# Thirteen output-gate column tiles move from the input projection into the delta-rule stage

## The reference, cut to what matters

```python
proj = h @ w_in
aq, ak, av, dqkv, dz, dbeta, da, gates = jnp.split(proj, SPLIT_IDX, axis=-1)
...
o = o_fwd + o_bwd          # gated delta rule, once in each direction
...
g_a, g_b = jnp.split(gates, 2, axis=-1)
merged = jax.nn.sigmoid(g_a) * (attn_out @ w_attn_branch) + jax.nn.sigmoid(g_b) * (dn_out @ w_dn_branch)
```

## Time and profile before

| | |
|---|---|
| median of the runs | 2925.03 us |
| the profiled execution | 2921.28 us |
| its span, first to last instruction | 2919.2 us |
| mean granted TensorE clock | 0.941 |
| TensorE busy | 2599.4 us (89%) |
| VectorE, ScalarE, GpSimd busy | 1047.7, 808.6, 583.3 us |
| projection | 0 to 740 us |
| attention | 740 to 1016 us |
| delta rule | 1016 to 1434 us |
| merge, mix_out | 1434 to 1826 us |
| ff_in, ff_out | 1826 to 2919 us |

### The profile page before, as it was taken

The page is one execution under the profiler, slowest core; times in us unless marked ns, Lnnn a source line. Parts: engine busy times, 40 slices in busy tenths (PEclk is TensorE's granted clock), DMA queues, the critical chain, the costliest instruction groups (busy, mean ns, idle before and its releaser), DMA issues. The chain is left out here.

```text
span 2919.2 us, 33331 instructions
## 1 busy us (share of the span) xinstructions
PE 2599.4 (89%) x12792; PEld 2174.6 (74%) x12792; DVE 1047.7 (36%) x1372; ACT 808.6 (28%) x1223; POOL 583.3 (20%) x498
## 2 busy tenths in 40 slices
PE   6999999999799862878669796999999979998998
PEld 5888887888577652878658585888888858887887
DVE  4675035000588755664454332100000032224333
ACT  4343223010577630111120132311111142223221
POOL 3352155221000050212142132212222100000000
PEclk9999999999899985888769898999999989999999
DMA  4223213421232293446465544332323164336442
GB/s 142 73 83 94 72 62 121 132 74 69 111 129 97 81 289 116 159 162 202 136 191 169 180 170 173 130 90 72 90 72 90 57 209 133 101 129 213 169 152 104
DMA packets 313805, 372.00 MB, mean 127 GB/s; under 512 B 51560, under 2 KB 248808, under 8 KB 309096
## 3 DMA queue, kind: packets, MB, share of 16 engines
q1 hardware_dynamic: 189368, 274.57, 28.7%
q10 hardware_dynamic: 124336, 96.05, 10.1%
HBM read 250.93 MB, written 119.64 MB: 127 GB/s over the span
## 5 line engine op out<-in xcount | busy, mean ns | idle before, releaser
L2165 DVE TENSOR_TENSOR hid_lo<-ff_raw,hid_hi 128x1024 fp32r<-128x1024 f32 x96 | 113.9, 1222 | 836.1 <-ACT hid_hi L2129 836.0
L2075 PE MATMUL y_ps<-w_hi,hid_hi 128*128 128x512 f32 x768 | 301.5, 393 | 30.7 <-DVE w_lo L2159 19.8
L2075 PE MATMUL y_ps<-w_lo,hid_hi 128*128 128x512 f32 x768 | 300.2, 391 | 0.0
L2075 PE MATMUL y_ps<-w_hi,hid_lo 128*128 128x512 f32 x768 | 300.1, 391 | 0.0
L115 PE MATMUL proj_ps<-ht_hi,win_hi 128*128 128x512 f32 x888 | 260.6, 402 | 0.0
L115 PE MATMUL proj_ps<-ht_lo,win_hi 128*128 128x512 f32 x888 | 251.3, 391 | 0.0
L115 PE MATMUL proj_ps<-ht_hi,win_lo 128*128 128x512 f32 x888 | 250.4, 390 | 0.0
L115 PE MATMUL ff_ps<-ffx_hi,w_hi 128*128 128x512 f32 x768 | 217.1, 391 | 16.9 <-DVE ffx_lo L1944 16.9
L115 PE MATMUL ff_ps<-ffx_lo,w_hi 128*128 128x512 f32 x768 | 216.6, 391 | 0.0
L115 PE MATMUL ff_ps<-ffx_hi,w_lo 128*128 128x512 f32 x768 | 216.3, 390 | 0.0
L2129 ACT ACTIVATE hid_hi<-ff_raw 128x1024 fp32r<-128x1024 f32 x96 | 97.4, 1053 | 355.2 <-PE y_ps L2075 329.5
(11 more groups left out here) (225 smaller groups left out, 4196.6 us busy)
## 6 DMA issues: line engine op xcount, KB each, us to landing
ff_raw<-s_hid_s SPq DMA_DIRECT2D x96, 512.0 KB, 4.4
pack_in<-s_dn_s SPq DMA_DIRECT2D x24, 1024.0 KB, 6.6
s_hid_s<-ff_stage ACTq DMA_DIRECT2D x32, 768.0 KB, 4.3
win_raw<-in_w_in SPq DMA_DIRECT2D x39, 512.0 KB, 3.7
w_raw<-in_w_ff_in SPq DMA_DIRECT2D x32, 512.0 KB, 5.3
ff_raw<-in_w_ff_out SPq DMA_DIRECT2D x32, 512.0 KB, 5.4
s_gate_s<-proj_stage ACTq DMA_DIRECT2D x16, 768.0 KB, 3.2
k_head<-s_k_s SPq DMA_DIRECT2D x8, 1536.0 KB, 8.0
```

What stands on the lines that cost most here:

```text
L2075: mm = pe.matmul(acc[:, bank(u, t)], x[:, (t if opens(t) else kh), k], y[:, w], start=w == 0 and first == 0, stop=w == KF - 1 and first == 2)
L2165: dve.tensor_tensor(hlo[:, b, ks].rearrange("p k j -> p (k j)"), raw[:, r], f32(hhi[:, b, ks]).rearrange("p k j -> p (k j)"), ALU.subtract ...
```

## The change

`project` keeps the first 3 gate tiles (`EARLY_GATES`), 26 tiles in all; `GATING` becomes 14. The activations `ht_hi`, `ht_lo` stay in SBUF through `deltanet`, which now follows at once; `attend` comes after it. `deltanet` computes the other 13 gate tiles: 13 x 3 groups ("units") of 24 matmuls, into two banks of PSUM in turn. The stage is a list of segments (`ORDER`): 11 makes, 4 waiting segments, make 11, 4 waiting segments, 25 steps. Each gets a number of fill matmuls (`FILL`), which `fill` issues at fixed places in the segment: before and after a make, and at five places between the links of a step. ScalarE loads the weights (one raw buffer), evacuates units by sigmoid and stores them; GpSimd splits the weights at the beginning of segments. A step now belongs to one direction: step v is direction v % 2, chunk step v // 2, and its links are woven with the preparation of step v+1, of the other direction. Packs, triangles, inverses and outputs have one buffer per direction instead of two; the two banks of the inverse's growth are shared by the directions, the gates' two banks in `make` are no longer doubled. The inverse of batch 1 begins with 12 rounds ahead of the steps and goes on with two rounds at each of two places of steps 0 to 4, batch 2 at steps 6 to 13. The identity that an inversion starts from is loaded by SP instead of copied by GpSimd. In SP's order the triangle and the inverse of step v+2 are loaded apart from its pack, and the first triangles and packs come after the last store of `make`.

```diff
-             [("gate", i, GATE_COL + i * P) for i in range(2 * KD)])
+             [("gate", i, GATE_COL + i * P) for i in range(EARLY_GATES)])
...
-    GATING = N - 8
+    GATING = 14
...
+    GATES = range(EARLY_GATES, 2 * KD)
+    UNIT = 3 * KD
+    ORDER = ([("make", t) for t in range(11)] + [("wait", n) for n in range(4)] + [("make", 11)] + [("wait", 4 + n) for n in range(4)] +
+             [("step", v) for v in range(-1, STEPS)])
+    FILL = {"make": 10, "wait": 24, "step": 25}
...
+        def at(v):
+
+            return v % 2, v // 2
...
+        PRE = 12
+        WOVEN = {}
+        for v in range(5):
+            j = PRE + 4 * v
+            WOVEN[v] = [(1, j, min(j + 2, BLK - 1)), (1, min(j + 2, BLK - 1), min(j + 4, BLK - 1))]
+        for v in range(6, 14):
+            j = 4 * (v - 6)
+            WOVEN[v] = [(2, j, min(j + 2, BLK - 1)), (2, min(j + 2, BLK - 1), min(j + 4, BLK - 1))]
...
+                for v in range(2):
+                    load_low(v)
+                for v in range(2):
+                    load_pack(v)
+                for v in range(STEPS):
+                    if v == 5:
                         store_inverse(1)
                         load_blocks(2)
+                        sp.wait_ge(s["inv_stored"], 128)
+                        load_identity()
+                    if v == 14:
                         store_inverse(2)
+                    if v + 2 < STEPS:
+                        load_low(v + 2)
+                        load_inverse(v + 2)
+                        load_pack(v + 2)
+                    store_out(v)
...
+                def fill(seg, share):
+
+
+                    end = filled[seg] + int(round((filled[seg + 1] - filled[seg]) * share))
+                    while place[0] < end:
+                        x, n = divmod(place[0], UNIT)
+                        i, g = divmod(x, NG)
+                        k, first = divmod(n, 3)
+                        if n == 0:
+                            pe.wait_ge(s["w_ready"], i + 1)
+                            if x >= 2:
+                                pe.wait_ge(s["f_used"], x - 1)
+                        w, h = ((whi, ht_hi), (whi, ht_lo), (wlo, ht_hi))[first]
+                        mm = pe.matmul(ps[:, 6 + x % 2], w[:, i % 2, k], h[:, k, g * 512:(g + 1) * 512], start=n == 0, stop=n == UNIT - 1)
+                        if n == UNIT - 1:
+                            mm.then_inc(s["f_done"], 1)
+                        place[0] += 1
...
+                    if kind == "make":
+                        fill(seg, 0.5)
+                        if n == 0:
+                            sums()
+                        make(n)
+                    if kind == "step":
+                        now, after = n >= 0, n + 1 < STEPS
...
                         if now:
+                            state_products(n)
                         if after:
+                            grow_x32(n + 1)
+                        fill(seg, 0.24)
                         if now:
+                            solve(n)
+                        fill(seg, 0.4)
                         if after:
+                            grow_t32(n + 1)
                         if now:
+                            new_products(n)
                         if after:
+                            turn(n + 1)
+                        fill(seg, 0.64)
                         if after:
+                            grow_x64(n + 1)
+                        fill(seg, 0.84)
                         if after:
+                            grow_r64(n + 1)
+                    fill(seg, 1)
...
+                        act.activation(sig[:, u], ps[:, 6 + u], ACT.Sigmoid).then_inc(s["f_used"], 1)
+                        act.wait_ge(s["f_used"], x + 1)
+                        act.dma_start(io["gate_s"][GATES[i] * P:(GATES[i] + 1) * P, g * 512:(g + 1) * 512], sig[:, u]).then_inc(gate_stored[u], 16)
...
+                    pool.tensor_copy(whi[:, i % 2], raw[:]).then_inc(s["w_hi"], 1)
+                    pool.wait_ge(s["w_hi"], i + 1)
+                    pool.tensor_tensor(wlo[:, i % 2], raw[:], f32(whi[:, i % 2]), ALU.subtract).then_inc(s["w_ready"], 1)
...
-PHASES = [project, attend, deltanet, merge, mix_out, ff_in, ff_out]
+PHASES = [attend, merge, mix_out, ff_in, ff_out]
...
+        project(nc, io, ht_hi, ht_lo)
+        deltanet(nc, io, ht_hi, ht_lo)
```

More of the change, by code:

```diff
@@ L953, in deltanet, with view @@
[L953 to L959, removed]
-        ps = c.ps("dn_ps", [P, 8, 512])
+        def view(first, shape, of=arena):
+            n = int(np.prod(shape))
+            names = "abcd"[:len(shape)]
+            return of[:, first:first + n].rearrange(f"p ({' '.join(names)}) -> p {' '.join(names)}", **dict(zip(names, shape)))
@@ new lines, in deltanet @@
+        feat = view(0, (3, 2, DNW))
+        decay = view(3072, (2, 2, NH, P))
+        made = arena[:, 5120:10240].rearrange("p (v a h t) -> p v a h t", v=2, a=5, h=NH)
+        other_masks = view(5120, (2, 2, P))
+        made_in = view(0, (2, 2, NH, P))
+        r, x_last, v_new, state = (view(1024 * n, (2, NH, P), late) for n in range(4))
+        q_state = view(3072, (2, NH, P))
+        out = view(4096, (2, DNW))
+        pack = view(5120, (2, 4, DNW))
+        x_m = view(9216, (NH, HALF))
@@ L970, in deltanet @@
[L970 to L978, removed]
+        pack_in, qk_back, low_back, inv_back, out_stored, state_ready, gate_stored = (c.sems2(n) for n in (
+            "pack_in", "qk_back", "low_back", "inv_back", "out_stored", "state_ready", "gate_stored"))
@@ L980, in side, with scaled @@
+        def at(v):
+            return v % 2, v // 2
+        def scaled(v):
+            return len([w for w in range(v) if not last(w // 2)])
         def side(a, which, b):
@@ L1044, in load_inverse @@
-                def load_inverse(u):
+                def load_inverse(v):
+                    d, u = at(v)
                     sp.wait_ge(s["inv_stored"], 64 * (u // 4 + 1))
                     if u == 0:
[L1047 to L1055, removed]
@@ L1189, in _, with low @@
[L1189 to L1196 removed]
+                    heads(ps[:, 2 + b], lambda h: feat[:, t % 3, 0, h * P:(h + 1) * P], lambda h: feat[:, t % 3, 1, h * P:(h + 1) * P]).then_inc(s["qk_mm"], 1)
+                def low(d):
+                    return lambda h: made_in[:, d, LOW, h]
@@ new lines, in turn, with grow_x64 @@
+                def turn(v):
+                    d, u = at(v)
+                    pe.wait_ge(s["t_upd"], v + 1)
+                    for h in range(NH):
+                        tr = pe.transpose(ps[:, BA, h * P:(h + 1) * P], inv_in[:, d, 0, h], ident[:])
+                    tr.then_inc(s["turned"], 1)
+                def grow_x64(v):
+                    d, u = at(v)
+                    heads(ps[:, BD], low(d), lambda h: side(inv_in[:, d, 0], d, HALF)[:, h], HALF).then_inc(s["x64_mm"], 1)
@@ L1272, in _ @@
+                for u in range(2):
+                    act.wait_ge(gate_stored[u], sent[u])
             @block.vector
@@ L1453, in _ @@
[L1453 to L1473 removed]
+                        pool.wait_ge(pack_in[d], 16 * (u + 1))
```

632 lines of the change are left out of this document (335 added, 297 removed).

## The result

The changed kernel takes 2813.02 us (median of four runs, 2810.65 to 2814.03), against 2926.56 us for the kernel before beside it: a ratio of 0.9608, with a 95% interval of 0.9586 to 0.963. The profiled execution took 2812.34 us, its span is 2810.6 us, and the mean granted clock of TensorE rose from 0.941 to 0.956.

A forecast was written before the change was run, and what follows sets the result against it. The prediction took TensorE as the bound, idle or at a lower clock in the delta-rule stage: 2921.3 - 212.2 + 102.1 + 1 gave 2812, plus 2 for the median, 2814 us; range 2776 to 2868.

The forecast's parts named there:

- Removed: Projection: the 13 moved gate tiles' whole 212.2 us goes; the moved gating block costs 1 us.
- Steps: Delta-rule steps: TensorE is the bound, fill covering each link's read-back; 14.45 us per step, 346.5 us in all.
- Inverse waits: Steps: TensorE waits 9.4 and 9 us for inverses of batches 1 and 2, slow matmuls 2.5 each; together 23 us.
- GpSimd beside VectorE: Steps: weight splits hold VectorE through the shared SBUF port, mostly covered by slack; 3 us.
- The stage's beginning: Delta-rule stage before the steps: split, load and later triangle loads move the first step matmul from 1150.55 to near 1156.5.
- The end: End of the delta-rule stage: 4.3 us to the next stage's first issue, as before.
- A: Delta-rule stage: the two inverse waits vanish and the start does not grow; 2782 us, chance 0.18.
- B: Shared SBUF port: all 13 splits in series with VectorE, and VectorE with TensorE; 2856 us, chance 0.11.
- C: Steps: TensorE's clock stays at the earlier mean of 0.85, adding 61 us; 2875 us, chance 0.10.
- D: Steps: fill covers no wait, one direction at a time exposes each link; period 19.0 us, 2965 us, chance 0.07.
- E: Delta-rule stage: fill merely lengthens it by its own 212 us; 2925 us, chance 0.04.

The follow-up runs named there:

- e3: Changed kernel with SP's wait for batch 1's inverse to land, and the identity load, moved behind the loads of step 7: 2810.22 us.
- e7: e3 with the loads of step 7's triangle and inverse also put ahead of batch 1's stores: 2803.05 us.
- e9: Changed kernel with GpSimd's subtraction of each weight split cut into four pieces: 2808.57 us.
- e5: Changed kernel with GpSimd's subtraction of each weight split performed twice: 2838.36 us.
- e1: Changed kernel with all 16 gate tiles back in the projection and no fill in the delta-rule stage: 2918.79 us, 0.997 of the kernel before.
- e10: Changed kernel with step 7's loads first, batch 2 earlier, more fill in waiting segments, subtraction in pieces, first split behind the first gate products: 2789.59 us.

## Why the prediction was right, point by point

**Forecast 2814, measured 2813.02.** The sum held because its large terms are of one kind: matmuls counted and priced by spacing. That it came within 1 us is luck: the start is 3.7 us and the end 2.8 us longer than in the sum, and the way from the first step's matmul to the last output is 6.4 us shorter (1046.99 - 678.40 = 368.6 against 375).

- *Removed, 212.2 us plus 1 for the gating block.* The last evacuation is at 529.01, 0.83 us later than tile 25 before. Right.
- *Steps, 14.45 us.* Measured 14.26 in quiet steps; TensorE is the bound there, as the sum took it. But the reason given, that fill covers each link's read-back, is only a small part: without fill a quiet step waits 0.61 us. The other direction's matmuls cover the links, one behind the other as well as in alternation: 8.46 us for one direction's own work stands against 8.48 in the kernel before and 9.42 in the new order without fill.
- *Inverse waits, 9.4 + 9 us and 2.5 behind each.* Measured 11.09 and 4.14; with the slow matmuls behind them the steps lost 28.61 - 14.26 = 14.35 and 19.36 - 14.26 = 5.1 us, 19.5 in all against 23. The first has the right place and a wrong reason: the step that waited (step 7) takes its inverse from batch 0, which was long in DRAM. The prediction's step that failed is "Batch 1 ends with step 4 and is first needed by the matmuls at the head of segment 6's second group"; what held is its second half, that loads queue on SP. SP's wait for the landing is not enough to explain it: without that wait (e3) the loads are held nearly as long behind the stores just issued, and only a place ahead of the stores (e7) frees them. The second was priced 5 us too high: the loads issue in 1.81 us and the matmuls start 1.5 us behind the last issue, where I took 3.7 and 5.7.
- *GpSimd beside VectorE, 3 us.* Measured two long steps, 1.96 and 1.40 us, both gone in e9. Right in size, and luckily so: seven splits fall into the steps, not nine, and e5 shows that the cover ends there.
- *The stage's beginning, +6.* Measured from the stage's first issue (534.87) to the first step's matmul (678.40): 143.5 us, against 133.9 before, +9.6. In e1, without fill, it is 131.8: fill and splits cost 11.7. They are, place by place, 3.2 us at make 0, 3.1 more by the start of batch 0's inversion, 2.9 in the inversion (26.2 us against 23.4), 2.7 up to make 11 (30.7 us from the turned copy against 28.0). The mis-sized term is the makes: "hidden behind the blocks" was wrong, since SP's block load follows the makes' stores and moves with them; VectorE still waits 8.28 us for it.
- *The end, 4.3 us.* Measured from the last output's state product (1042.77) to the next stage's first issue (1054.13): some 24 fill matmuls and the output's store. From the last output (1046.99), where the 4.3 us were taken, it is 7.1: fill, a sigmoid and a gate store come behind it. The stage is 519.3 us long; predicted 519.1.

**Rivals.** A did not come: both waits are there, and the start grew. B is refuted for this kernel (3.4 us) but comes near when splits get twice as long (e5). C: the clock is 0.97 in the steps, not 0.85. It fell only behind a gap: in the window around the first wait (782 to 797 us) it is 0.64. D: the link waits that it feared are hardly there even without fill (period 9.42, where it asked for 19 with fill). E: 106 of the 212 us are saved (e1's 2919 us against 2813), and 2919 instead of 2819 shows that the fill is not merely added.

What stays open: whether the loads behind batch 1's stores were held by the order in their queue or by the load on the DMA engines, and what of e10's longer start is due to which edit.

## What to carry to other kernels

Independent matmuls are worth moving to a stretch in which TensorE idles or runs at a lower clock: here 63 of 76 us were free ahead of the steps, while a step that was already full paid 85% of its fill, and its last matmuls in full. So the next one belongs where the windows show idle time. After such a move look for what it queues behind on every engine: a load whose data has long been there kept TensorE waiting for 10 us behind stores that the same engine had just issued (e3), and putting it ahead of them takes an edit of a few lines. A long GpSimd operation beside a busy VectorE is best cut into pieces.

## What the runs showed of the hardware that I had not expected

- Four 32 KB loads issue in 1.94 us (after, at 783.62) and 2.05 us (e7, at 764.79), and in 7.96 us right behind seven transfers of 256 KB (e3, at 776.52).
- A GpSimd subtraction holds one VectorE operation with both inputs in SBUF (2.47 us instead of 0.42); two subtractions hold two (2.47 and 2.46, e5), and four short ones let an operation in between each (0.83, e9). An operation that reads PSUM beside SBUF took its usual 0.42 us in the middle of a subtraction (after, `late<-late,dn_ps` at 941.12).
- A wait of 3 us costs more than itself: behind it (e5, at 723.09) eight matmuls take 2.07 us instead of 1.05, and the step lost 6.1 us.
